# Neighbourhood attention: unscaled weights as the stationary side, sums applied by ScalarE on the way out, and two bias tables that exchange their homes

## The chip, the cores and the metric

The kernel runs on one core of a Trainium2 chip. A core has a matrix engine (TensorE, PE in the rows; its loads of the stationary operand are PEld), VectorE (DVE), ScalarE (ACT), GpSimd (POOL) and a queue that issues transfers (SyncE, SP), with 16 DMA engines behind it. The metric is the time of the program on the device in microseconds (us), the median of several runs. Everything is 32-bit floating point; the trace records each matmul of such operands as two passes.

## The reference

The program is two transformer blocks over 1024 tokens of 1024 features. The part that matters here is half of the second block's mixer:

```python
def neighbourhood_attention(q, k, v, rpb):      # B, T, H, dh = 1, 1024, 8, 64; a grid of 16 rows of 64 tokens
    ...
    scores = jnp.einsum('bhrqd,bhrikd->bhrqik', qg, k_rows) * (dh ** -0.5)   # a row's 64 queries, 8 rows of keys
    scores = jnp.where(in_win[...], scores + bias[None], -jnp.inf)
    p = jax.nn.softmax(scores.reshape(B, H, R, W, KH * W), axis=-1).reshape(B, H, R, W, KH, W)
    return jnp.einsum('bhrqik,bhrikd->bhrqd', p, v_rows)
```

It stands between a gated linear attention in both directions (its other half) and the output projection with the MLP behind it. The softmax divides each query's weights by their sum; that can be done before or after the product with the values.

## The kernel before

The instructions of each engine are written out in a fixed order. The work around the change is written as generators, one per stream of work and engine; `interleave` runs all streams of an engine one step at a time, and `pause(n)` lets a stream skip n steps, so the pauses set the order in which an engine meets the work of different units.

A **unit** is one row of the grid (64 queries) for one pair of heads: 128 partitions (two heads of 64 queries) by 512 keys. There are 16 rows and 4 pairs, 64 units. Eight streams n = 0 to 7 work at once, each with a PSUM bank, a tile of scores `n_sc` and small numbers `n_st`; n below 4 takes the even rows of pair n, the others the odd rows of pair n - 4. Eight units are a **round**, and there are eight rounds. In `near_head` the odd rows have their two heads crossed over, so the four score products of a pair's two units (64 by 64 stationary, 512 columns streamed) lie in the four quarters of the array. Crossed heads need a bias table with its halves exchanged, the turned table.

A unit's chain before: TensorE scores (`near_scores_tensor`, line 3498), VectorE adds the bias, negates and takes the minimum (3462), ScalarE takes the exponential and its sum (3443), VectorE inverts the sum (3465), GpSimd multiplies the weights by it (3480), TensorE turns them in four transposes (line 232, called from `near_values_tensor`), VectorE copies them out (3468), TensorE multiplies them with the values (3519: stationary 128x128 values, 128 turned columns streamed, two heads at once with halves of the result unused), and ScalarE copies the two used quarters of 64x64 over the queries (3449), which is the layout that the output projection reads. A score product of the next round waits for that copy (`mix_out`).

The loads are in `near_loads`, on SyncE's queue: at its end the bias table of the even rows (3136), the values shifted by one row (3138, two halves, for windows that begin at an odd row), and the turned table in two halves of 64 partitions (3142). The even rows' table lies over memory in use until the last projection unit of this attention (`unit_made`), the turned one at U_AT + 96 KB over `la`, the gates of the linear attention, in use until their last prefix sums (`sums_made`, line 3336). VectorE waits for both tables ahead of the attention (top of `neighbourhood`). The weights of the output projection (3740) are issued behind the point where the engines meet (`k.meet()`).

## Time and profile before

| | us |
|---|---|
| median of 3 runs | 3066.36 (3061.49 to 3067.91) |
| the profiled execution | 3066.58 |
| its span, first to last instruction | 3064.4 |
| TensorE busy | 2869.7 (94%) |
| VectorE, ScalarE, GpSimd busy | 1175.4, 596.9, 720.3 |
| mean granted TensorE clock | 0.974 of full speed |
| the neighbourhood attention | 2013.05 to 2171.41 |

Durations come from the one profiled execution. A group's busy time is the union of its instructions, so where they overlap it is below count times mean. "Idle before" names what ended the idle time ahead of an instruction. The clock is a share of 2.4 GHz. In rows of the trace a number behind x counts passes, two for each matmul and one for each transpose; in rows of the program's order it counts instructions.

### The profile page before, as it was taken

To read this page: it belongs to the slowest core of one execution; us is meant where nothing else is said; L and a number is where in the kernel's file an instruction comes from. 1 tells how busy PE (TensorE), PEld (TensorE's weight loads), DVE (VectorE), ACT (ScalarE), POOL (GpSimd) and SP (SyncE) were. 2 spreads that over 40 slices of the span, in tenths; PEclk is the share of its full clock that TensorE was granted. 3 is DMA by queue.
4 is the path that set the end of the run, shared out by engine and by line. 5 is a ranking of instruction groups with operands and counts; after the bars stand their busy time and mean duration, and the time that the engine had idled before them with its cause. 6 is when DMAs were issued, how large, how long until landed. Compare 5 with 4: busy or idle time off the path is not lost.

```text
span 3064.4 us, 30810 instructions
## 1 busy us (share of the span) xinstructions
PE 2869.7 (94%) x12130; PEld 1695.6 (55%) x12130; DVE 1175.4 (38%) x1999; ACT 596.9 (19%) x1223; POOL 720.3 (24%) x544
## 2 busy tenths in 40 slices
PE   7999998988988999999789999969999999999998
PEld 5886544888446666666444455537544444444443
DVE  6715777665132111111143145446633314133142
ACT  4001232322121221121232211125230000000001
POOL 3214565553211000000020000137521122111220
PEclk9999999999998999999899999979999999999999
DMA  8724494000237999999661100040201101111101
GB/s 264 232 45 52 97 249 111 1 28 29 112 137 317 395 426 426 424 426 390 245 221 38 55 1 15 14 132 1 90 28 55 53 30 41 41 55 45 38 28 55
DMA packets 180278, 417.08 MB, mean 136 GB/s; under 512 B 30676, under 2 KB 103828, under 8 KB 170904
## 3 DMA queue, kind: packets, MB, share of 16 engines
q1 hardware_dynamic: 163705, 372.49, 34.3%
q10 hardware_dynamic: 10512, 25.69, 2.6%
q0 software_dynamic: 5904, 16.78, 1.5%
q8 instruction: 101, 1.65, 0.2%
q14 instruction: 56, 0.46, 0.0%
HBM read 374.29 MB, written 59.88 MB: 142 GB/s over the span
## 4 chain that ended last, share of the span: by engine, by line
PE 86%; DVE 6%; DMA 2%; issue 2%; ACT 1%; POOL 1%; SPq 1%; POOLq 0%; ACTq 0%; DVEq 0%
PE bank L3809 27%; PE bank L2554 9%; PE bank L2557 8%; PE bank L748 6%; PE bank L2984 5%; PE bank L1946 4%; PE bank L3161 3%; PE bank L232 3%; PE bank L1266 3%; PE bank L3159 2%; PE bank L883 2%; PE bank L3519 1%; PE bank L1844 1%; PE bank L1841 1%; PE bank L1834 1%
## 5 line engine op out<-in xcount | busy, mean ns | idle before, releaser
L3809 PE MATMUL bank<-w_ff,uT 128*128 128x512 f32 x640 | 276.0, 592 | 0.0
L3809 PE MATMUL bank<-hT,w_ff 128*128 128x512 f32 x512 | 224.3, 596 | 4.3 <-DVE hT L3612 4.3
L3932 DVE TENSOR_TENSOR x_out<-x_out,bank 128x512 f32<-128x512 f32 x140 | 94.7, 687 | 291.5 <-PE bank L3809 291.3
L3809 PEld LDWEIGHTS bank<-w_ff,uT 128*128 128x128 f32 x640 | 121.6, 190 | 153.1 <-issue 153.1
L2554 PE MATMUL bank<-e_w,e_xsT 128*128 128x256 f32 x832 | 184.3, 382 | 1.6 <-DVE e_xsT L2640 1.6
L2557 PE MATMUL bank<-e_w,e_xsT 128*64 128x256 f32 x1408 | 160.8, 388 | 18.5 <-issue 18.5
L2554 PEld LDWEIGHTS bank<-e_w,e_xsT 128*128 128x128 f32 x832 | 158.1, 191 | 32.5 <-issue 11.3
L2984 PE MATMUL bank<-w_gla,nT 128*128 128x512 f32 x384 | 167.1, 595 | 2.4 <-ACT nT L2946 1.3
L3809 PEld LDWEIGHTS bank<-hT,w_ff 128*128 128x128 f32 x512 | 97.5, 191 | 126.3 <-issue 126.0
L3809 PE MATMUL bank<-h_sum,w_ff 128*128 128x512 f32 x384 | 166.1, 592 | 0.0
L2557 PEld LDWEIGHTS bank<-e_w,e_xsT 128*64 128x64 f32 x1408 | 113.2, 140 | 69.8 <-issue 31.2
L2711 DVE TENSOR_TENSOR e_hid<-e_act,bank 128x256 f32<-128x256 f32 x48 | 20.2, 421 | 337.7 <-PE bank L2554 170.4
L3873 POOL TENSOR_TENSOR w_ff<-w_ff,w_ff 128x2048 f32<-128x2048 f32 x9 | 42.7, 4746 | 355.7 <-PE bank L3809 352.5
L3809 PEld LDWEIGHTS bank<-h_sum,w_ff 128*128 128x128 f32 x384 | 73.0, 190 | 91.8 <-issue 91.8
L2984 PEld LDWEIGHTS bank<-w_gla,nT 128*128 128x128 f32 x384 | 72.7, 191 | 92.0 <-issue 88.3
L3161 PE MATMUL bank<-nT,w_nqk 128*128 128x512 f32 x256 | 121.8, 606 | 0.0
L3919 DVE TENSOR_TENSOR uT<-uT,bank 128x512 f32<-128x512 f32 x48 | 33.1, 689 | 229.1 <-PE bank L3809 229.0
L2493 POOL DMA_INDIRECT e_rows<-xn_rows,e_idx x25 | 25.0, 1001 | 405.9 <-PE bank L2523 380.1
L3846 ACT ACTIVATE uT<-bank 128x512 f32<-128x512 f32 x48 | 28.3, 600 | 468.9 <-PE bank L3809 468.9
L748 PE MATMUL bank<-w_in,hT 128*128 128x256 f32 x512 | 115.1, 383 | 0.0
L3480 POOL TENSOR_SCALAR n_sc<-n_sc,n_st 128x512 f32<-128x512 f32 x64 | 99.7, 1564 | 58.3 <-DVE n_st L3465 58.1
L3809 PE MATMUL bank<-w_ff,u_sum 128*128 128x512 f32 x256 | 110.5, 592 | 0.0
(530 smaller groups left out, 4805.1 us busy)
## 6 DMA issues: line engine op xcount, KB each, us to landing
e_w<-in_w SPq DMA_DIRECT2D x108, 2048.0 KB, 22.1
w_ff<-in_w_ff SPq DMA_DIRECT2D x32, 1024.0 KB, 5.2
y_rows<-zero SPq DMA_DIRECT2D x8, 3008.0 KB, 19.0
wa_rest<-in_w_ada SPq DMA_DIRECT2D x32, 512.0 KB, 5.3
y_rows<-e_y ACTq DMA_DIRECT2D x24, 512.0 KB, 9.3
wa<-in_w_ada SPq DMA_DIRECT2D x16, 512.0 KB, 10.8
w_qkv<-in_w_in SPq DMA_DIRECT2D x24, 256.0 KB
w_gla<-in_w_in SPq DMA_DIRECT2D x3, 2048.0 KB, 20.8
```

The source lines that it names most:

```text
L232: t = k.nc.tensor.transpose(bank[:, h * P:(h + 1) * P], src[:, h * P:(h + 1) * P], k.c("ident"))
L748: t = pe.matmul(out, still[:, f, g * P:(g + 1) * P], moving[:, f, :], start=step in (0, 1, 3) and g % 2 == f == 0, stop=f == 3, skip_group ...
L883: t = pe.matmul(k.bank[6 + m % 2][:, :], hT[:, f, m * P:(m + 1) * P], wz[:, f, :], start=f == 0, stop=f == NK - 1)
L1266: t = pe.matmul(conv_bank(k, p, step)[:, :], weights[step][:, f, :], tokens[step](f), start=step in (0, 1, 3) and f == 0, stop=f == 3, ski ...
L1946: t = pe.matmul(k.bank[2 * (m % 2) + h][:, :], mixed, b.w[h][:, f, :], start=f == 0, stop=f == NK - 1)
L2554: return pe.matmul(out, xT, weights[0], start=start, stop=stop)
L2557: t = pe.matmul(out[tokens, :], xT[:, tokens], w, start=start, stop=stop)
L2984: t = pe.matmul(k.bank[3 * (i % 2) + j][:, :], b.nT[:, f, i * P:(i + 1) * P], b.w[at][:, f, :], start=f == 0, stop=f == NK - 1)
L3161: t = pe.matmul(bank[:, :], wqk[c // 2 % 2][:, f, c % 2 * P:(c % 2 + 1) * P], nT[:, f, h * BANK:(h + 1) * BANK], start=f == 0, stop=f == N ...
L3480: g.tensor_scalar(b.sc[n][:, :], b.sc[n][:, :], b.st[n][:, 2:3], None, ALU.mult).then_inc(*s.weights_ready.up().inc)
L3809: t = pe.matmul(bank[:, :], still, moving, start=step in (0, 1, 3) and f == 0, stop=f == 3, skip_group_check=True)
L3932: v.tensor_tensor(dst, dst, k.bank[4 * ((ph + step) % 2) + g][:, :], ALU.add).then_inc(*s.added.up().inc)
```

## The change

1. The weights are turned unscaled, right behind the exponential. GpSimd's part goes.
2. The values product changes sides: the turned weights are the stationary operand (64 queries of one head at a time), the values are streamed (64 features), and the result has queries on its partitions: 8 matmuls a unit in the two column halves of the array, instead of 4 over all of it.
3. ScalarE copies this 128x64 result to a new tile `n_out` and scales it by the inverse sums; TensorE turns it back by two products of 64x64 with the identity; ScalarE copies that, 128x64 in one instruction, over the queries.
4. The bias tables exchange homes: the even rows' table goes to U_AT + 96 KB and is loaded once the last prefix sums of both directions are made; the turned one goes to the other place and is loaded ahead of the shifted values. VectorE waits for each table only at the first unit that reads it.
5. The pauses are new: a round has 12 steps (`NEAR_ROUND`) where it had 8.

```diff
@@ near_areas
-    ... for j, at in enumerate((N_AT + 16 * KB, U_AT + 96 * KB))],
+    ... for j, at in enumerate((U_AT + 96 * KB, N_AT + 16 * KB))],
@@ near_loads
+    for way in gla_s:
+        sy.wait_ge(*way.sums_made(NT))
+    sy.dma_start(near.bias[0][:, :, :], bias_rows).then_inc(*d.bias_got.up().inc)
     sy.wait_ge(*d.unit_made(NT + 4 * PAIRS))
     sy.wait_ge(*d.unit_out(NT))
-    sy.dma_start(near.bias[0][:, :, :], bias_rows).then_inc(*d.bias_got.up().inc)
+    for lo in (0, W):
+        sy.dma_start(near.bias[1][W - lo:P - lo, :, :], bias_rows[lo:lo + W, :, :]).then_inc(*d.bias_turned_got.up().inc)
     ... (the two loads of val_odd, as before)
-    for way in gla_s:
-        sy.wait_ge(*way.sums_made(NT))
-    for lo in (0, W):
-        sy.dma_start(near.bias[1][W - lo:P - lo, :, :], bias_rows[lo:lo + W, :, :]).then_inc(*d.bias_turned_got.up().inc)
@@ neighbourhood
-    k.nc.vector.wait_ge(*d.bias_got(1))
-    k.nc.vector.wait_ge(*d.bias_turned_got(2))
@@ near_start
-    return pause(2 * (n % PAIRS) + n // PAIRS)
+    return pause(NEAR_ROUND // PAIRS * (n % PAIRS) + n // PAIRS)
@@ near_scalar
-        yield from pause(4)
+        yield from pause(2)
         a.wait_ge(*s.neg_max(u + 1))
         a.activation(sc[:, :], sc[:, :], ACT.Exp, scale=-1.0, bias=st[:, 0:1], accum_out=st[:, 1:2]).then_inc(*s.exp_ready.up().inc)
-        yield from pause(4)
+        yield from pause(6)
+        a.wait_ge(*s.sum_inverse(u + 1))
         a.wait_ge(*s.av_made(u + 1))
-        for h in range(2):
-            values, queries = near_head(n, h)
-            m = s.mix_out.up() if h else k.A.up()
-            a.activation(b.qkT[values, p, i * W:(i + 1) * W], k.bank[n][values, queries], ACT.Copy).then_inc(*m.inc)
+        a.activation(b.out[n][:, :], k.bank[n][:, 0:W], ACT.Copy, scale=st[:, 2:3]).then_inc(*s.o_ready.up().inc)
+        yield from pause(2)
+        a.wait_ge(*s.o_turned(u + 1))
+        a.activation(b.qkT[:, p, i * W:(i + 1) * W], k.bank[n][:, W:2 * W], ACT.Copy).then_inc(*s.mix_out.up().inc)
+        yield from pause(2)
@@ near_vector
+        elif u < 2:
+            v.wait_ge(*(d.bias_turned_got(2) if u else d.bias_got(1)))
@@ near_gpsimd: gone
@@ near_values_tensor
-        yield from pause(6)
-        pe.wait_ge(*s.weights_ready(u + 1))
+        yield from pause(4)
         pe.wait_ge(*s.neg_max(u + 1))
+        pe.wait_ge(*s.exp_ready(u + 1))
         transposes(k, bank, b.sc[n]).then_inc(*s.rows_turned.up().inc)
-        yield from pause(2)
+        yield from pause(3)
...
         for q in range(4):
-            t = pe.matmul(bank[:, 0:P], val[:, lo // 2 + q, p * P:(p + 1) * P], b.sc[n][:, q * P:(q + 1) * P], start=q == 0, stop=q == 3)
+            for h in range(2):
+                features, queries = near_head(n, h)
+                t = pe.matmul(bank[queries, 0:W], b.sc[n][:, q * P + queries.start:q * P + queries.stop], val[:, lo // 2 + q, p * P + features.start:p * P + features.stop],
+                              start=q == 0, stop=q == 3)
         t.then_inc(*s.av_made.up().inc)
+        yield from pause(2)
+        pe.wait_ge(*s.o_ready(u + 1))
+        for h in range(2):
+            features, queries = near_head(n, h)
+            t = pe.matmul(bank[features, W:2 * W], b.out[n][queries, :], k.c("ident")[queries, queries], start=True, stop=True)
+        t.then_inc(*s.o_turned.up().inc)
+        yield from pause(3)
```

**TensorE in the middle of the attention, before.** Rows are instructions in the program's order; `n_sc_1_18324` to `18327` are the weights of streams 0 to 3 and `18328` to `18331` those of streams 4 to 7, line 3498 is a pair's scores, line 232 the transposes, line 3519 the values product:

```order
L232 MATMUL bank<-consts_49,n_sc_1_18328 128x128 x4
L3519 MATMUL bank<-n_sc_1_18331,n_val_even_18320 128x128 x4
L3519 MATMUL bank<-n_sc_1_18324,n_val_even_18320 128x128 x4
L232 MATMUL bank<-consts_49,n_sc_1_18325 128x128 x4
L3498 MATMUL bank<-n_qkT_18319 64x512 x4
L3519 MATMUL bank<-n_sc_1_18328,n_val_odd_18321 128x128 x4
L232 MATMUL bank<-consts_49,n_sc_1_18329 128x128 x4
L3519 MATMUL bank<-n_sc_1_18325,n_val_even_18320 128x128 x4
L232 MATMUL bank<-consts_49,n_sc_1_18326 128x128 x4
L3498 MATMUL bank<-n_qkT_18319 64x512 x4
L3519 MATMUL bank<-n_sc_1_18329,n_val_odd_18321 128x128 x4
```

**The same place after the change.** Line 3487 is the scores, 3510 the values product, 3517 the turn back; `n_out_1_18332` to `18335` are the results of streams 0 to 3, `18336` to `18339` those of streams 4 to 7:

```order
L3510 MATMUL bank<-n_val_even_18320,n_sc_1_18324 64x64 x8
L232 MATMUL bank<-consts_49,n_sc_1_18325 128x128 x4
L3517 MATMUL bank<-consts_49,n_out_1_18339 64x64 x2
L3510 MATMUL bank<-n_val_odd_18321,n_sc_1_18328 64x64 x8
L232 MATMUL bank<-consts_49,n_sc_1_18329 128x128 x4
L3517 MATMUL bank<-consts_49,n_out_1_18332 64x64 x2
L3487 MATMUL bank<-n_qkT_18319 64x512 x4
L3517 MATMUL bank<-consts_49,n_out_1_18336 64x64 x2
L3510 MATMUL bank<-n_val_even_18320,n_sc_1_18325 64x64 x8
L232 MATMUL bank<-consts_49,n_sc_1_18326 128x128 x4
L3510 MATMUL bank<-n_val_odd_18321,n_sc_1_18329 64x64 x8
L232 MATMUL bank<-consts_49,n_sc_1_18330 128x128 x4
```

Before, transposes and values products, both over the whole array, stand next to each other between the scores. Now the values products have another shape, and a turn back of two small products stands two or three rows behind each of them, around the scores.

**SyncE's queue at the end of the linear attention, before.** `w_nqk` is the last projection weight of this attention, `n_bias_1_18322` the even rows' table, `n_bias_1_18323` the turned one:

```order
L3133 DMA w_nqk_1_19204<-in_w_in 128x8x256
L3136 DMA n_bias_1_18322<-bias_rows 128x3840
L3138 DMA n_val_odd_18321<-n_val_even_18320 64x4096
L3138 DMA n_val_odd_18321<-n_val_even_18320 64x3584
L3142 DMA n_bias_1_18323<-bias_rows 64x3840 x2
```

**And after the change**, with the waits of the diff ahead of the first and the second table:

```order
L3133 DMA w_nqk_1_19212<-in_w_in 128x8x256
L3136 DMA n_bias_1_18322<-bias_rows 128x3840
L3140 DMA n_bias_1_18323<-bias_rows 64x3840 x2
L3142 DMA n_val_odd_18321<-n_val_even_18320 64x4096
L3142 DMA n_val_odd_18321<-n_val_even_18320 64x3584
```

The turned table has moved ahead of the shifted values; the even rows' table stands where it stood, but waits for something earlier.

## Rows read from the trace of the kernel before

**Rows 1.** stretches: busy us of PE, PEld, DVE, ACT, POOL; PEclk, DMA share, GB/s
```profile
2013.05:2037.72 24.67, 3.69 (x17) 0.80 (x17) 2.78 (x10) 2.73 (x7) 1.64 (x2) 0.50 1.01 247
2037.72:2042.50 4.78, 4.78 (x21) 2.84 (x22) 2.13 (x6) 0.31 (x2) 3.06 (x2) 0.50 1.05 409
2042.50:2171.41 128.91, 123.03 (x990) 91.00 (x989) 84.07 (x243) 75.98 (x248) 95.01 (x61) 1.00 0.01 2
2171.41:3064.40 892.99, 874.71 (x2080) 390.01 (x2080) 306.74 (x328) 73.12 (x136) 184.24 (x68) 0.99 0.14 48
```

**Rows 2.** chain of waits, 1990 to 2200 us: start, us, what
```profile
2008.51 25.32 DMA n_bias<-bias_rows
```

**Rows 3.** timeline, start of the stage: start, us, engine, line, what, idle before
```profile
2034.08 0.69 DVE L3462 CUSTOM_DVE_ANT_0 n_sc<-bank,n_bias 128x512 f32<-128x512 f32 x1 [22.70 <-DMA n_bias<-bias_rows]
2037.72 1.11 PE L232 MATMUL bank<-consts,n_sc 128*128 128x128 f32 x4 [20.98 <-POOL n_sc L3480]
```

**Rows 4.** timeline of TensorE, one round
```profile
2051.64 0.65 PE L232 MATMUL bank<-consts,n_sc 128*128 128x128 f32 x4 [0.64 <-POOL n_sc L3480]
...
2062.05 0.60 PE L232 MATMUL bank<-consts,n_sc 128*128 128x128 f32 x4
2062.48 1.06 PE L3519 MATMUL bank<-n_sc,n_val_even 128*128 128x128 f32 x8
2063.38 0.60 PE L232 MATMUL bank<-consts,n_sc 128*128 128x128 f32 x4
2063.91 1.09 PE L3498 MATMUL bank<-n_qkT 64*64 64x512 f32 x8
2064.93 1.16 PE L3519 MATMUL bank<-n_sc,n_val_even 128*128 128x128 f32 x8
2065.92 0.60 PE L232 MATMUL bank<-consts,n_sc 128*128 128x128 f32 x4
2066.42 1.16 PE L3519 MATMUL bank<-n_sc,n_val_even 128*128 128x128 f32 x8
2068.22 0.66 PE L232 MATMUL bank<-consts,n_sc 128*128 128x128 f32 x4 [0.64 <-POOL n_sc L3480]
```

**Rows 5.** groups by line, 2013 to 2172 us: busy us, mean ns, idle before
```profile
L3480 POOL TENSOR_SCALAR n_sc<-n_sc,n_st 128x512 f32<-128x512 f32 x64 | 99.7, 1564 | 58.3 <-DVE n_st L3465 58.1
L3443 ACT ACTIVATE n_sc<-n_sc,n_st 128x512 f32<-128x512 f32 x64 | 46.0, 720 | 23.4 <-DVE n_st L3462 21.9
L3462 DVE CUSTOM_DVE_ANT_0 n_sc<-bank,n_bias 128x512 f32<-128x512 f32 x64 | 43.7, 684 | 45.2 <-DMA n_bias<-bias_rows 22.7 <-PE bank L3498 22.2 <-issue 0.3
L3468 DVE COPY n_sc<-bank 128x512 f32<-128x512 f32 x64 | 43.4, 687 | 17.4 <-PE bank L232 17.4
L3449 ACT ACTIVATE n_qkT<-bank 64x64 f32<-64x64 f32 x128 | 27.9, 218 | 56.0 <-PE bank L3519 54.0
```

**Rows 6.** short and half-width passes elsewhere: page, timelines, one line's instructions
```profile
L3809 PE MATMUL bank<-w_ff,uT 128*128 128x512 f32 x640 | 276.0, 592 | 0.0
...
1101.21 7.09 PE L2557 MATMUL bank<-e_w,e_hidT 128*64 128x512 f32 x32
1108.23 0.48 PE L2554 MATMUL bank<-e_w,e_xsT 128*128 128x256 f32 x1
...
1130.43 0.20 PEld L2557 LDWEIGHTS bank<-e_w,e_xsT 128*64 128x64 f32 x4 [0.76 <-issue]
...
L1292 PE MATMUL bank<-consts,abT x8: 201/202/223, 358.5 to 358.7; 8*128 8x8 f32 x8
```

**Rows 7.** instructions of the prefix sums: duration ns min/median/max, first and last start
```profile
L3336 PE MATMUL bank<-consts,la x64: 167/251/251, 1764.5 to 1982.4; 128*128 128x2 f32 x64
```

**Rows 8.** landing of line 3136; stretches: us, PEclk, DMA share, GB/s
```profile
DMA to landing us min/median/max: 8.7/8.7/8.7
...
2009.00:2012.00 3.00, 0.97 1.11 415
2024.00:2027.00 3.00, 0.50 1.02 215
```

More of the change, by code:

```diff
@@ L3069 @@
 NEAR_RATE = 1.8
-Near = namedtuple("Near", "qkT val_even val_odd bias sc st")
+Near = namedtuple("Near", "qkT val_even val_odd bias sc out st")
 def gla_tile(k, n):
@@ L3113, in near_areas @@
     return Near(k.at("n_qkT", U_AT + 48 * KB, P, 2 * PAIRS, T), k.at("n_val_even", U_AT + 80 * KB, P, NT, BANK), k.at("n_val_odd", N_AT, P, NT, BANK),
-                [k.at(f"n_bias{j}", at, P, PAIRS, (2 * KH - 1) * W) for j, at in enumerate((N_AT + 16 * KB, U_AT + 96 * KB))],
-                n_sets("sc", U_AT + 112 * KB, NSETS, KH * W), n_sets("st", EARLY_AT + 4 * KB, NSETS, 8))
+                [k.at(f"n_bias{j}", at, P, PAIRS, (2 * KH - 1) * W) for j, at in enumerate((U_AT + 96 * KB, N_AT + 16 * KB))],
+                n_sets("sc", U_AT + 112 * KB, NSETS, KH * W), n_sets("out", EARLY_AT, NSETS, W), n_sets("st", EARLY_AT + 4 * KB, NSETS, 8))
 def near_unit_of(u):
@@ L3395, in neighbourhood @@
 def neighbourhood(k, d, b):
[L3397 to L3399 removed]
+    s = k.on("scored neg_max exp_ready sum_inverse rows_turned pT_out av_made o_ready o_turned mix_out")
     interleave(*(near_scalar(k, s, b, n) for n in NEAR_ORDER))
[L3401 to L3402 removed]
+    interleave(*(near_vector(k, s, d, b, n) for n in NEAR_ORDER))
     interleave(*(near_values_tensor(k, s, d, b, n) for n in NEAR_ORDER), *(near_scores_tensor(k, s, b, p) for p in range(PAIRS)))
@@ L3457, in near_vector @@
         _, dr = near_window(i)
-        yield from pause(3)
+        yield
         v.wait_ge(*s.scored(u // 2 + 1))
@@ L3461, in near_vector @@
             v.wait_ge(*s.av_made(u - NSETS + 1))
+        elif u < 2:
+            v.wait_ge(*(d.bias_turned_got(2) if u else d.bias_got(1)))
         v.tensor_tensor_reduce(sc[:, :], k.bank[n][:, :], b.bias[n // PAIRS][:, p, dr * W:(dr + KH) * W], -1.0, -NEG, ALU.add, ALU.min, st[:, 0:1]).then_inc(*s.neg_max.up().inc)
-        yield from pause(2)
+        yield from pause(3)
         v.wait_ge(*s.exp_ready(u + 1))
         v.reciprocal(st[:, 2:3], st[:, 1:2]).then_inc(*s.sum_inverse.up().inc)
-        yield from pause(2)
+        yield
         v.wait_ge(*s.rows_turned(u + 1))
         v.tensor_copy(sc[:, :], k.bank[n][:, :]).then_inc(*s.pT_out.up().inc)
-        yield
-def near_gpsimd(k, s, b, n):
-    g = k.nc.gpsimd
-    yield from near_start(n)
-    for u, _, _ in near_rows(n):
-        yield from pause(5)
-        g.wait_ge(*s.exp_ready(u + 1))
-        g.wait_ge(*s.sum_inverse(u + 1))
-        g.tensor_scalar(b.sc[n][:, :], b.sc[n][:, :], b.st[n][:, 2:3], None, ALU.mult).then_inc(*s.weights_ready.up().inc)
-        yield from pause(3)
+        yield from pause(7)
 def near_scores_tensor(k, s, b, p):
     pe = k.nc.tensor
-    yield from pause(2 * p)
+    yield from pause(NEAR_ROUND // PAIRS * p)
     for r in range(ROWS // 2):
-        yield from pause(2)
         if r:
@@ L3499, in near_scores_tensor @@
         t.then_inc(*s.scored.up().inc)
-        yield from pause(6)
+        yield from pause(NEAR_ROUND)
 def near_values_tensor(k, s, d, b, n):
@@ L3509, in near_values_tensor @@
         val = b.val_odd if lo % 2 else b.val_even
-        yield from pause(6)
-        pe.wait_ge(*s.weights_ready(u + 1))
+        yield from pause(4)
         pe.wait_ge(*s.neg_max(u + 1))
+        pe.wait_ge(*s.exp_ready(u + 1))
         transposes(k, bank, b.sc[n]).then_inc(*s.rows_turned.up().inc)
-        yield from pause(2)
+        yield from pause(3)
         pe.wait_ge(*s.pT_out(u + 1))
```

7 lines of the change are left out of this document (3 added, 4 removed).

## The prediction

> **What bounds the kernel now.** I read the stretches of the stage by window first, then the chain of waits through it, then TensorE's timeline of one round, then the groups by line. The whole change lies in the neighbourhood attention, from 2013.05 us (the engines meet behind the gated linear attention) to 2171.41 us (first product of the output projection). What follows, 892.99 us with TensorE busy 874.71 of them, starts when the attention ends and only shifts with it [rows 1].
>
> The attention has two parts with different limits. From 2013.05 to 2037.72 us TensorE is busy 3.69 of 24.67 us: it makes the scores of two pairs and then stands [rows 1]. The chain says why: 25.32 us of a transfer of the bias table [rows 2]. VectorE's first instruction on scores starts at 2034.08, after a wait of 22.70 us for it, and TensorE's first turn of weights at 2037.72 [rows 3]. From there on TensorE is the bound: 123.03 of 128.91 us busy at full clock [rows 1]. Its timeline repeats in rounds of 16.58 us (2051.64 to 2068.22), with one gap in each: the transposes at 2068.22 waited 0.64 us for GpSimd [rows 4], which scales the weights, 1.56 us a unit [rows 5]. From 2066.42 to 2068.22 TensorE does 0.90 us of products, so a round loses 0.90 us and holds 15.68 us of work.
>
> **What that work is made of.** Steps between starts in [rows 4]: four transposes between work of the same shape 0.43 us (2062.05 to 2062.48), the values product of a unit 0.90 us (2062.48 to 2063.38; 8 passes, 0.111 each), a pair's scores 1.02 us (2063.91 to 2064.93). The scores are two waves of a 512-column pass, and such a pass is 0.431 us (276.0 over 640 [rows 6]), so 0.86. The rest is the price of using the array in another shape: transposes ahead of scores take 0.53 instead of 0.43, scores 1.02 instead of 0.86, products behind scores 0.99 instead of 0.90 (2064.93 to 2065.92). That is 0.35 us for two changes, 0.175 each. The experts' half-width work shows 7.02 us for 32 passes in two column halves (1101.21 to 1108.23), 16 x 0.431 = 6.90 for the streaming, so 0.12 for a way out [rows 6]. I take 0.16 per change, bounds 0.10 and 0.175. The same 32 passes show that two column halves do run side by side.
>
> **The change, part by part.**
> *The start.* The table of the even rows waits now only for the last prefix sums of both directions, 1982.4 us [rows 7], instead of 2006.3; it took 8.7 us to land [rows 8], so it is there by 1992, under the linear attention. The turned table is issued at 2006.3 with nothing ahead of it. It moves at half the speed of the full one: 415 GB/s while the full table runs, 215 while a turned half runs [rows 8]. Its 1.97 MB take 9.2 us; with 1 us before the first packet and 1.5 us behind the last it lands at about 2018.0. Bounds: 2015.0, if it moved like the full one, and 2025, if the odd values, issued right behind, took half of the engines. Odd values and projection weights come behind it; the first odd row is two rounds away, so they are hidden. The first unit needs the early table alone: its transposes can start at about 2016.9 (scores 1.9 at the slow clock, reduction 0.7, exponential 0.9, signals). The second needs the turned one: reduction 2018.1 to 2018.8, exponential to 2019.6 [rows 5], transposes at 2019.7. Dense work thus starts at 2019.7 instead of 2037.72: 18.0 us won.
> *The clock* is at 0.50 when the stage opens and rose 4.8 us after the work had become dense (2037.72 to 2042.50) [rows 1]. The same 4.8 us, a loss of 2.4, come again: no gain, no loss.
> *GpSimd's 64 multiplications go.* They were on the path once a round: 0.90 us back, against new small waits for which I allow 0.2. VectorE inverts the sums as before.
> *The values product* becomes 8 instructions a unit, 16 passes in 8 pairs, the two of a pair in the two column halves, with 64 stationary and 64 streamed columns each. No such pass is in the trace. From below: half of a 128-column pass, 0.055 us a pair. From above: 0.111 a pair, as a pass of today, if the halves don't overlap. Near: eight passes of 8 streamed columns, alternating between two row groups, start within 0.2 us (358.5 to 358.7), 0.07 a pair at most, and four loads of 64 columns, two per half, are over in 0.20 us, the length of one included [rows 6]. I take 0.06: 0.48 us a unit, 3.84 a round, where there were 8 x 0.89 = 7.1.
> *The turn back* is added: 2 instructions, two pairs of small passes, 0.12 us a unit, 0.96 a round.
> *Changes of shape.* The new order [the order rows in the section on the change] alternates full width (transposes), half width (values) and quarters (scores, turn back). Over a full round of it I count 22 changes, before 8: 22 x 0.16 = 3.52 us.
> A round: scores 4 x 0.86 = 3.44, transposes 8 x 0.43 = 3.44, values 3.84, turn back 0.96, changes 3.52: 15.2 us of work, 15.4 with the new waits. (Before: 3.44 + 3.44 + 7.1 + 8 x 0.175 = 15.4, measured 15.68.) The cheaper products pay for the changes of shape and for little more.
> *ScalarE* had an exponential and two 64x64 copies a unit (0.72 and 2 x 0.218 [rows 5]); now the copies are 128x64, which I price 0.23 (bounds 0.218 and 0.30). Some 1.2 us a unit, 9.4 a round, lie under TensorE's 15.4; VectorE's reduction and copy, 0.684 each, stay. The chain of a unit (scores 1.1, reduction 0.7, exponential 0.9, transposes 0.6, copy 0.7, values 0.8, scaled copy 0.4, turn 0.4, copy 0.4) is 6 us plus signals, and the order leaves a twelfth of a round, 1.3 us, or more at each hand-over. Uncovered, a late copy costs its 0.23 us at each of 64 turns, 15 us; that is how B below comes about.
>
> **The sum.** 8 rounds x 15.2 = 121.6, less the first transposes and two scores, done by 2019.7 (2.6): 119.0. Plus 2.4 clock, 1.6 new waits, 2.0 for the tail. The end comes at 2019.7 + 125.0 = 2144.7 instead of 2171.4: 26.7 us less. The same count for before, 2037.72 + 8 x 15.68 - 2.6 + 2.4 + 7 x 0.90 = 2169.3, leaves 2.1 for its tail, so the way of counting closes. The profiled execution took 3066.58 us (span 3064.4, 2.2 around it), 0.2 above the median of 3066.36. Forecast: 3066.4 - 26.7 = 3040.
>
> **Rivals.**
> A. *The column halves don't overlap in such short passes.* A pair then costs 0.111, at 80 pairs a round 4.1 us more, 32.6 over 8 rounds: 5.9 us slower than now, 3072. It decides from 0.10 us a pair on, where the 26.7 are used up. For it: four queued instructions in 0.06 us, which no row shows sustained. Against: [rows 6].
> The Trainium skill, "TensorE: Matmul & The Clock Gate", LDWEIGHTS, prices a load by its columns, 53 ns for 64; loads in single file would make 107 ns a pair and this rival. The four loads in 0.20 us speak against single file.
> B. *The longer chain holds the round at its old length.* ScalarE's queue has the scaled copy and the last copy between exponentials, and TensorE waits for both. If that eats all of the round's gain, 8 x (16.58 - 15.4) = 9.4 us come back: 3049.
> C. *The turned table lands at 2025*: 7 us come back: 3047.
> D. *A floor per pass adds up.* 96 more passes a round (160 against 64), at 0.025 us each (eight starts within 0.2 us [rows 6]): 2.4 us a round, 19 in all: 3059. For it: the passes are as short as any in the trace. Against: those eight stream 8 columns each and cost the floor and no more, so it reads as a floor under a pass, not on top of it.
> The skill's "TensorEngine Tiling", Instruction Overhead, is this rival's rule: some 60 cycles for each matmul, and no tiling of a dimension that is small already.
>
> **How the numbers follow.** Forecast 0.58, A 0.11, B 0.16, C 0.08, D 0.07. The lower end: 0.055 a pair and 0.10 a change give a round of 13.5, 14 us less than forecast: 3026. Both upper bounds together give 3077, which is A and more. The range 3026 to 3064 takes in B, C and D and leaves out A and a little. A measurement of this kernel tells 0.2%, 6 us, from no change. Faster by more (below 3060.2): forecast, B, C and part of D, less what I may have missed: 0.85; within 0.05; slower 0.10.
>
> **What would show it.** VectorE's first reduction near 2015 us and the second near 2018, with a DMA wait of 2 to 3 us between; nothing on GpSimd; rounds of about 15.4 us with TensorE busy throughout; values passes in pairs 0.06 us apart; ScalarE's 128x64 copies near 0.23 us. I am wrong if pairs lie 0.11 us apart, if ScalarE is the releaser of TensorE in each round, if the granted clock falls below 1.0 inside the stage, or if dense work starts after 2022.

## The result, and the profile after

The changed kernel takes 3037.39 us (median of 4 runs, 3036.02 to 3037.81) against 3067.14 for the kernel before on the same chip (3061.49 to 3068.89): ratio 0.9905, 95% interval 0.989 to 0.9921, so 29.7 us or 1% less. The forecast was 3040 us.

The first view is the same as in [rows 1], the stage cut at the places that answer to those of before: opening to the first transposes of unit 1, from there to the clock's return, the rest, and what follows. Columns: window, its length, busy time (instructions) of PE, PEld, DVE, ACT, POOL, then PEclk, DMA share, GB/s.

```profile
2018.64:2025.22 6.58, 4.44 (x21) 1.37 (x21) 2.40 (x8) 1.78 (x5) 0.00 (x0) 0.68 1.01 206
2025.22:2029.60 4.38, 4.38 (x36) 2.46 (x38) 2.42 (x9) 2.39 (x7) 0.00 (x0) 0.62 1.03 217
2029.60:2142.38 112.78, 112.21 (x1740) 76.86 (x1738) 83.26 (x242) 70.45 (x245) 0.00 (x0) 1.00 0.12 42
2142.38:3035.30 892.92, 874.53 (x2080) 390.12 (x2080) 306.72 (x328) 73.03 (x136) 184.38 (x68) 0.99 0.14 48
```

The stage takes 123.74 us (2018.64 to 2142.38) instead of 158.36, 34.6 less. What follows is as long as before. The span shrank by only 29.1 us because this execution opened the stage 5.6 us later. 3.7 of these are there long before the changed code: the experts' first products, line 2557, start at 1000.1 us instead of 996.4. In the 14 profiled executions of the two kernels and the experiments they start between 994.6 and 1011.1 us, and the stage opens between 2012.49 and 2029.42 (four of the experiments also move the opening by their own edit, as told there). Whether such a shift belongs to the execution or to the program isn't shown: the four runs of the changed kernel lie within 1.8 us of each other. A median carries some microseconds of this, so below I compare the length of the stage as well. It comes from one profiled execution of each kernel; how well it repeats wasn't measured, but kernels with the same operations in the same order have the same rounds (14.68 us in two of them, 16.57 and 16.58 in two others).

The start, in the timelines of VectorE and TensorE of the changed kernel (start, us, engine, line, what, idle before and its releaser), answers to [rows 3]:

```profile
2020.81 0.69 DVE L3464 CUSTOM_DVE_ANT_0 n_sc<-bank,n_bias 128x512 f32<-128x512 f32 x1 [4.14 <-PE bank L3487]
2023.52 0.69 DVE L3464 CUSTOM_DVE_ANT_0 n_sc<-bank,n_bias 128x512 f32<-128x512 f32 x1 [2.02 <-DMA n_bias<-bias_rows]
```

And TensorE's, over the same microseconds:

```profile
2018.64 3.69 PE L3487 MATMUL bank<-n_qkT 64*64 64x512 f32 x16 [0.81 <-ACTq L164]
2022.56 0.74 PE L232 MATMUL bank<-consts,n_sc 128*128 128x128 f32 x4 [0.23 <-ACT n_sc L3441]
2025.22 0.63 PE L232 MATMUL bank<-consts,n_sc 128*128 128x128 f32 x4 [1.91 <-ACT n_sc L3441]
```

The 22.70 us for the table have become 2.02 for its turned half, and dense work begins 6.58 us after the opening instead of 24.67. A piece of a steady round (14.68 us from 2063.60 to the same place at 2078.28) answers to [rows 4]:

```profile
2063.60 0.28 PE L3517 MATMUL bank<-consts,n_out 64*64 64x64 f32 x2
2063.62 0.65 PE L3487 MATMUL bank<-n_qkT 64*64 64x512 f32 x2
2063.71 0.23 PE L3517 MATMUL bank<-consts,n_out 64*64 64x64 f32 x2
2063.76 1.03 PE L3487 MATMUL bank<-n_qkT 64*64 64x512 f32 x6
2064.53 0.29 PE L3517 MATMUL bank<-consts,n_out 64*64 64x64 f32 x4
2064.75 0.69 PE L3510 MATMUL bank<-n_val_even,n_sc 128*64 128x64 f32 x16
2065.36 0.66 PE L232 MATMUL bank<-consts,n_sc 128*128 128x128 f32 x4
2065.95 0.69 PE L3510 MATMUL bank<-n_val_odd,n_sc 128*64 128x64 f32 x16
...
2068.86 0.33 PE L3517 MATMUL bank<-consts,n_out 64*64 64x64 f32 x4
2069.12 0.69 PE L3510 MATMUL bank<-n_val_even,n_sc 128*64 128x64 f32 x16
```

No row has a gap in brackets. TensorE never waits in a round; the 0.57 us missing from 112.78 in the third row of the first view are two waits at the very end. A values product takes 0.61 us from its start to the next work's (2064.75 to 2065.36) where [rows 4] has 0.90. Pass by pass, its two column halves start within 7 ns of each other, and the pairs follow each other by 58 ns, 107 behind the first. The turn back's first passes start at 2063.60, the scores' at 2063.62 and its next at 2063.71, although they stand ahead of the scores in the queue: the two run among each other. Scores and two turn backs together take 1.15 us (2063.60 to 2064.75) where scores alone take 1.02, and a turn back between other work 0.26 (2068.86 to 2069.12), which has one more change of shape in it.

TensorE's clock, in a finer cut of the first two rows (columns as in the first view):

```profile
2022.50:2025.22 2.72, 0.75 (x5) 0.57 (x5) 1.70 (x6) 0.96 (x3) 0.00 (x0) 0.94 0.95 193
2025.22:2026.20 0.98, 0.98 (x8) 0.59 (x12) 0.98 (x5) 0.56 (x2) 0.00 (x0) 1.00 1.32 267
2026.20:2029.60 3.40, 3.40 (x32) 1.86 (x26) 1.44 (x5) 1.83 (x5) 0.00 (x0) 0.50 0.95 202
```

It rose to 2.4 GHz early in the first of these rows, behind 3.69 us of scores and before the work was dense. It fell back to 1.2 GHz 1 us after the dense work had begun, behind TensorE's wait of 1.91 us, stayed there for 3.4 us, and was up from then on.

The groups of the stage, answering to [rows 5] (busy us, mean ns, idle before):

```profile
L3441 ACT ACTIVATE n_sc<-n_sc,n_st 128x512 f32<-128x512 f32 x64 | 46.0, 719 | 26.0 <-DVE n_st L3464 24.1
L3445 ACT ACTIVATE n_out<-bank,n_st 128x64 f32<-128x64 f32 x64 | 19.8, 309 | 19.5 <-PE bank L3510 18.8 <-DVE n_st L3467 0.8
L3448 ACT ACTIVATE n_qkT<-bank 128x64 f32<-128x64 f32 x64 | 13.3, 211 | 3.6 <-PE bank L3517 3.6
L3517 PE MATMUL bank<-consts,n_out 64*64 64x64 f32 x256 | 19.9, 237 | 0.2 <-ACT n_out L3445 0.2
```

The scaled copy takes 309 ns, more than either copy of before; the idle time beside it is ScalarE waiting for TensorE, so it hides.

### The profile page after: what moved, and what is told of

The parts are those of the page before. It is cut to its first block, busy times and chain, and to the rows that moved or that the text cites. A ratio compares the mean times of both kernels' runs of the same rounds, so it can differ in the third digit from the quotient of the medians.

```text
span 3035.3 us, 32282 instructions
## 1 busy us (share of the span) xinstructions
PE 2865.1 (94%) x12898; PEld 1687.8 (56%) x12898; DVE 1179.5 (39%) x1999; ACT 592.7 (20%) x1223; POOL 618.4 (20%) x480
## 4 chain that ended last, share of the span: by engine, by line
PE 88%; DVE 6%; issue 2%; DMA 2%; ACT 1%; POOL 1%; SPq 0%; ACTq 0%; DVEq 0%; POOLq 0%
PE bank L3808 28%; PE bank L2554 9%; PE bank L2557 8%; PE bank L748 6%; PE bank L2984 5%; PE bank L1946 4%; PE bank L3161 3%; PE bank L232 3%; PE bank L1266 3%; PE bank L3159 2%; PE bank L883 2%; PE bank L1844 1%; PE bank L3510 1%; PE bank L1841 1%; PE bank L1834 1%
## 5 line engine op out<-in xcount | busy, mean ns | idle before, releaser
L2554 PEld LDWEIGHTS bank<-e_w,e_xsT 128*128 128x128 f32 x832 | 158.5, 192 | 32.7 <-issue 11.3
L748 PEld LDWEIGHTS bank<-w_in,hT 128*128 128x128 f32 x512 | 97.8, 192 | 14.9 <-issue 1.7
## 6 DMA issues: line engine op xcount, KB each, us to landing
y_rows<-zero SPq DMA_DIRECT2D x8, 3008.0 KB, 18.8
```

The source lines that it names most:

```text
L748: t = pe.matmul(out, still[:, f, g * P:(g + 1) * P], moving[:, f, :], start=step in (0, 1, 3) and g % 2 == f == 0, stop=f == 3, skip_group ...
L2554: return pe.matmul(out, xT, weights[0], start=start, stop=stop)
```

## The experiments

For each I give the median and, from its profiled run, the length of the stage (first scores to the output projection's first product).

**One half of the change each.** The bias tables alone, put on the kernel before:

```diff
+    for way in gla_s:
+        sy.wait_ge(*way.sums_made(NT))
+    sy.dma_start(near.bias[0][:, :, :], bias_rows).then_inc(*d.bias_got.up().inc)
     sy.wait_ge(*d.unit_made(NT + 4 * PAIRS))
...
+        elif u < 2:
+            v.wait_ge(*(d.bias_turned_got(2) if u else d.bias_got(1)))
```

> The kernel before with the bias tables' part of the change alone: homes exchanged, the even table loaded early, the turned one ahead of the odd values, VectorE's waits moved to units 0 and 1. Theory: the two parts add up, and this one is worth what the first transposes come earlier. They start 24.67 us after the stage opens before and 6.58 us after it in the changed kernel, so the stage (158.36 us before) becomes about 140.3, and the time 3067.1 - 18 = 3049 us (3046 to 3052). The rounds stay at 16.58 us with GpSimd's waits in them. Rival: the long start lets later units catch up (all scores are there when the tables land), so an early table only spreads the first round's work and wins at most what TensorE stood idle; the stage then becomes 148 or more and the time 3055 or more.

Measured: 3051.82 us (3049.17 to 3053.59), ratio 0.9939 (0.9923 to 0.9956). Its timeline:

```profile
2014.34 3.69 PE L3498 MATMUL bank<-n_qkT 64*64 64x512 f32 x16 [0.81 <-ACTq L164]
2021.98 1.12 PE L232 MATMUL bank<-consts,n_sc 128*128 128x128 f32 x4 [3.95 <-POOL n_sc L3480]
...
2155.22 14.00 PE L3809 MATMUL bank<-w_ff,n_qkT 128*128 128x512 f32 x32 [0.58 <-ACTq L164]
```

The stage is 140.88 us, 17.5 less than before, and the steady rounds are the old 16.57. Theory right by the stage and the rounds. The other half, the changed kernel with homes, loads and waits as before:

```diff
-    for way in gla_s:
-        sy.wait_ge(*way.sums_made(NT))
-    sy.dma_start(near.bias[0][:, :, :], bias_rows).then_inc(*d.bias_got.up().inc)
     sy.wait_ge(*d.unit_made(NT + 4 * PAIRS))
     sy.wait_ge(*d.unit_out(NT))
+    sy.dma_start(near.bias[0][:, :, :], bias_rows).then_inc(*d.bias_got.up().inc)
...
+    k.nc.vector.wait_ge(*d.bias_got(1))
+    k.nc.vector.wait_ge(*d.bias_turned_got(2))
```

> The changed kernel with the bias tables' homes, loads and waits as they were before: the unscaled weights, the product with column halves, the scaling copy and the turn back alone. Theory: the start stays as before (first transposes 24 to 25 us after the opening), the rounds are 14.68 us long instead of 16.58 and the tail 7.8 instead of 11.9, so the stage is 158.4 - 7 x 1.9 - 4.1 = 141 us and the time about 3050 us (3046 to 3054). Rival: the prediction's forecast of 15.4 us a round was right and the shorter round of the changed kernel comes from the staggered start that the two tables give (scores and turn backs beside each other because the units are apart in time); with all units starting together rounds are 15.4 or longer, and the time is 3056 or more.

Measured: 3056.13 us (3054.84 to 3060.13), ratio 0.9955 (0.9938 to 0.9971). The stage is 141.43 us (2019.27 to 2160.70), 16.9 less than before, with rounds of 14.68: as expected, while the median is 2 us over the range. The stage doesn't explain that; this execution opened it at 2019.27, 6.2 us later than the kernel before. The two halves add up: 17.5 + 16.9 = 34.4 of the 34.6.

**Do the two column halves run side by side?** The loops exchanged, so that neighbours in the queue share a half:

```diff
-        for q in range(4):
-            for h in range(2):
-                features, queries = near_head(n, h)
+        for h in range(2):
+            features, queries = near_head(n, h)
+            for q in range(4):
```

> The changed kernel with the loops of the values product exchanged: first the four passes of one head, then the four of the other, so that passes next to each other lie in the same half of the columns. The output is unchanged. Theory: the two halves of a pair run side by side (a pair takes 0.058 us, a pass alone 0.055 or more), and one after the other they cost 8 x 0.055 instead of 4 x 0.058 in a unit: 0.21 us more, 1.7 in a round, 13 in the stage: 3050 us (3045 to 3055). If a pass in one half costs 0.111, 0.65 a unit and 3079 us. Rival (cost goes by the columns alone, nothing runs side by side: a pass costs 0.029 wherever it lies): 3037 us, no change.

Measured: 3056.6 us (3056.12 to 3062.02), ratio 0.9959 (0.9945 to 0.9973); stage 143.17 us, 19.4 more than the changed kernel's, rounds 16.92. From its timeline:

```profile
2079.87 0.97 PE L3510 MATMUL bank<-n_val_even,n_sc 128*64 128x64 f32 x16
2080.76 0.66 PE L232 MATMUL bank<-consts,n_sc 128*128 128x128 f32 x4
```

The same 16 passes take 0.89 us instead of 0.61: 0.28 a unit. The rival (cost by columns alone) is out. The passes of one half start 0.058 us apart, which is what a pair takes in two halves. I had counted 8 passes where there are 16: with 16, full single file would have been 0.46 a unit more. It came out at 0.28 because this order isn't full single file either: the second head's passes begin 0.29 us behind the first head's (2079.87 and 2080.16), with three of the first's still to start. Even so the narrow product now costs what the wide one did before (0.90, [rows 4]; 0.15 of the 0.89 is the change of shape behind it): all the product wins is the company of the other half.

**Is it the turned side, or the width?** The kernel before with the product in halves and nothing else:

```diff
-            t = pe.matmul(bank[:, 0:P], val[:, lo // 2 + q, p * P:(p + 1) * P], b.sc[n][:, q * P:(q + 1) * P], start=q == 0, stop=q == 3)
+            for h in range(2):
+                features, queries = near_head(n, h)
+                t = pe.matmul(bank[features, queries], val[:, lo // 2 + q, p * P + features.start:p * P + features.stop],
+                              b.sc[n][:, q * P + queries.start:q * P + queries.stop], start=q == 0, stop=q == 3)
```

> The kernel before with nothing but its values product cut in column halves: values stay the stationary side, now 64 features of one head at a time, against 64 columns of that head's weights; GpSimd's multiplication, ScalarE's two copies and the tables' start stay. The product of a unit goes from 4 passes of 128x128 (0.222 us each) to 8 of 128x64 (0.058 a pair). Theory: what the change saves in the product is the width, not the turned side; TensorE's own work in a round falls from 15.68 to about 13.5 us. GpSimd's multiplications take 8 x 1.56 = 12.5 us of it and stand in each unit's chain, so some of the gain turns into waits: a round of 14 to 15.2 us, 7 x 2 = 14 us less in the stage: 3053 us (3046 to 3058). Rival: the units' chains through GpSimd set the round already (its waits are 0.9 us a round before), and the freed time becomes waiting: 16.4 us a round and 3065 us or more.

Measured: 3064.07 us (10 runs, 3059.5 to 3069.72), ratio 0.9981 (0.9968 to 0.9993); stage 148.41, 10.0 less than before, rounds 15.30. Between theory and rival, and the median above the theory's range: of the stage's 10.0 us only some 5 arrived in it, and this execution opened the stage at 2026.43. Its timeline says why:

```profile
2077.97 0.69 PE L3521 MATMUL bank<-n_sc,n_val_even 128*64 128x64 f32 x16 [0.22 <-DVE n_sc L3468]
2079.77 0.66 PE L232 MATMUL bank<-consts,n_sc 128*128 128x128 f32 x4 [1.12 <-POOL n_sc L3480]
```

TensorE's product is as short as in the changed kernel (0.69 for x16), so the width makes it short and not the turned side. But the waits for GpSimd grew from 0.90 to some 1.6 us a round (here 1.19 between 2078.58 and 2079.77, and 0.43 at another unit), and VectorE's copy adds 0.3. They eat part of what the width frees.

**GpSimd's place by itself.** In the kernel before the multiplication is cut to 8 columns; the weights are therefore not scaled:

```diff
-        g.tensor_scalar(b.sc[n][:, :], b.sc[n][:, :], b.st[n][:, 2:3], None, ALU.mult)
+        g.tensor_scalar(b.sc[n][:, 0:8], b.sc[n][:, 0:8], b.st[n][:, 2:3], None, ALU.mult)
```

> The kernel before with GpSimd's multiplication cut from 512 columns to 8 (all else, waits too, stays; the output isn't scaled). It prices GpSimd's place in the chain alone. Theory: TensorE's waits for GpSimd go (0.90 us in each of 7 steady rounds, 3 to 4 us in the tail, 1.5 at the start), TensorE's own 15.68 us a round stay: the stage is 10 to 12 us shorter, 3058 us. Rival (the unit's chain through VectorE and ScalarE takes GpSimd's place, as the wait's last entry): rounds stay above 16.2 us and the time above 3064.

Measured: 3058.31 us (6 runs, 3056.2 to 3061.04), ratio 0.9968 (0.9956 to 0.998); stage 148.94, 9.4 less; rounds 15.62, and no wait for GpSimd after the first. The 0.90 us a round were real (16.57 to 15.62 is 0.95), and nothing took its place; the stage won a little less than the 10 to 12 us of the theory.

**The turn back's price.** In the changed kernel each is done twice:

```diff
-        for h in range(2):
+        for h in (0, 1, 0, 1):
```

> The changed kernel with each turn back done twice in a row (the second writes the same numbers). It prices the turn back's passes without its changes of shape. Theory: half of the turn backs start beside the scores and the pairs follow each other every 0.055 to 0.1 us; two more pairs are 0.11 to 0.2 us a unit, less where they lie beside the scores: 0.8 to 1.2 us a round, 6 to 9 us: 3045 us. Rival A: they vanish beside the scores, under 2 us in all: 3037 to 3039. Rival B: the turn back is as dear as its isolated 0.26 us shows: 2.1 a round, 16 us: 3053.

Measured: 3051.95 us (3048.67 to 3057.03), ratio 0.9941 (0.9924 to 0.9958); stage 131.43, 7.7 more than the changed kernel's; rounds 15.68, 1.00 more, so 0.125 us for the second turn back of a unit. Theory right by the stage and the round. The second turn back costs about the same everywhere: 0.11 to 0.14 us beside the scores (a visit with one unit's turn back is 1.24 us for 1.13, with two units' 1.42 for 1.15), 0.12 between other work (0.38 for 0.26). So the scores hide part of a first turn back, and next to nothing of a second. The median is 7 us higher than the stage explains; the profiled run, the slowest of the four at 3057.03, opened at 2029.42, the latest of all, and the other three are 3 to 8 us faster.

**Changes of shape, and a better order.** The changed kernel's operations in another order (a table of slots in place of the pauses), two products, two transposes, two turn backs and the scores for each pair:

```diff
+NEAR_ROUND = 24
+NEAR_SLOTS = {"bias": (2, 3), "exp": (4, 6), "inverse": (5, 7), "turn": (10, 11), "turned": (10, 12), "values": (14, 15), "scale": (15, 17), "back": (18, 18), "out": (20, 21)}
```

> The changed kernel with all its operations, in another order: the two units of a pair side by side, so that TensorE runs scores, two values products, two transposes, two turn backs for each pair, in place of alternating. Theory (a change of shape costs 0.10 to 0.16 us on TensorE): four changes fewer from product to transposes and four fewer from transposes to product in a round, 8 x 0.14 = 1.1 us less: 13.6 us a round, stage 8 us shorter, 3029 us (3026 to 3033). Rival: TensorE runs into VectorE and ScalarE, whose work now comes in pairs (8 x 1.61 = 12.9 and 8 x 1.43 = 11.4 us a round), and stands idle for what it saves: 3037 or more.

Measured: 3029.01 us (3026.91 to 3031.43), ratio 0.9869 (0.9853 to 0.9886); stage 112.25, rounds 13.02. One pair:

```profile
2073.82 0.69 PE L3521 MATMUL bank<-n_val_even,n_sc 128*64 128x64 f32 x16
2074.34 0.64 PE L3521 MATMUL bank<-n_val_odd,n_sc 128*64 128x64 f32 x16
2074.90 1.09 PE L232 MATMUL bank<-consts,n_sc 128*128 128x128 f32 x8
2075.93 0.34 PE L3528 MATMUL bank<-consts,n_out 64*64 64x64 f32 x8
2076.09 1.04 PE L3497 MATMUL bank<-n_qkT 64*64 64x512 f32 x8
2077.06 0.69 PE L3521 MATMUL bank<-n_val_even,n_sc 128*64 128x64 f32 x16
```

The theory's mechanism is right and its size was too small: the round is 1.66 us shorter and the stage 11.5, where it had 1.1 and 8. It counted eight changes fewer; the rows show ten, since the turn backs lie beside the scores in every pair: 22 become 12, and 10 x 0.16 is 1.6. That the median is the forecast 3029 is luck: this execution opened the stage at 2021.59, 2.9 us later than the changed kernel's. And the same order with the values stationary in halves, scaling by GpSimd and no turn back:

```diff
+                t = pe.matmul(bank[features, 0:W], val[:, lo // 2 + q, p * P + features.start:p * P + features.stop],
+                              b.sc[n][:, q * P + queries.start:q * P + queries.stop], start=q == 0, stop=q == 3)
...
+        a.activation(b.qkT[:, p, i * W:(i + 1) * W], k.bank[n][:, 0:W], ACT.Copy).then_inc(*s.mix_out.up().inc)
```

> The bias tables as in the changed kernel, but the weights scaled by GpSimd and the values as the stationary side, in column halves, both heads' results in one 64-column stretch (so one copy by ScalarE and no turn back); and TensorE's order in each pair of units is scores, both values products, both transposes, instead of alternating. Theory: TensorE needs 1.09 us for two products in a row (as the halves-only kernel's trace has it), about 1.03 for two units' transposes and 1.0 for the scores, so 3.15 a pair and 12.6 a round; VectorE then has 8 x (0.68 + 0.08 + 0.15 + 0.69) = 12.9 us of work in a round and GpSimd 12.5, so VectorE binds at 12.9 to 13.4 instead of TensorE's 14.68. 7.5 rounds' worth x 1.5 = 11 us: about 3026 us (3022 to 3032). Rival (GpSimd in the chain): three engines within 3% of each other and 1.56 us of GpSimd between exponent and transposes make waits of 1.5 us a round or more, as in the halves-only kernel (1.4), and the time is 3037 or more.

Measured: 3023.65 us (3022.71 to 3025.2), ratio 0.9852 (0.9836 to 0.9869), the fastest of all: 13.7 us under the changed kernel by the medians, 13.5 by the stage (110.21); rounds 12.50. One pair of it on TensorE:

```profile
2072.15 1.09 PE L3507 MATMUL bank<-n_qkT 64*64 64x512 f32 x8
2073.17 0.69 PE L3531 MATMUL bank<-n_sc,n_val_even 128*64 128x64 f32 x16
2073.68 0.64 PE L3531 MATMUL bank<-n_sc,n_val_odd 128*64 128x64 f32 x16
2074.25 1.09 PE L232 MATMUL bank<-consts,n_sc 128*128 128x128 f32 x8
2075.27 1.09 PE L3507 MATMUL bank<-n_qkT 64*64 64x512 f32 x8
```

And 70 us of steady rounds (columns as in the first view):

```profile
2050.00:2120.00 70.00, 70.00 (x1068) 46.03 (x1065) 61.31 (x180) 39.54 (x134) 69.51 (x46) 1.00 0.01 2
```

A period is 3.12 us without a gap. 8 units of 8 pairs at 0.058 (3.71) + 3.44 for scores + 3.44 for transposes are 10.59; the other 1.91 of the round's 12.50 are 12 changes of shape at 0.16. The changed kernel's own steps show the same price: a product takes 0.61 us for 0.46 of passes, four transposes 0.59 for 0.43, scores 1.02 for 0.86. 20 changes between transposes, products and scores make 3.2, and 10.59 + 3.2 leave 0.89 of its 14.68 for 8 turn backs with all their own changes. By the timeline it is 1.00: six beside the scores add 0.47 to four visits of 1.02, two between other work take 0.26 each. In the paired order a round with turn backs is 0.52 longer than one without (13.02 against 12.50): 0.065 a unit, two units' turn backs side by side in four quarters, just ahead of the scores. My expectation named VectorE as the next bound, from a sum of durations; it is busy 61.31 of 70, and GpSimd, at 69.51, is the engine that is nearly full. It holds nobody up: the order leaves a third of a round (8 slots of 24) between its multiplication and the transposes.

**The start: attempts, none of use.** First, the projections that run beside the gated attention handed out faster:

```diff
-NEAR_RATE = 1.8
+NEAR_RATE = 2.0
```

> The changed kernel with one number changed: the projections that fill the gated attention's gaps are handed out 2.0 a step instead of 1.8, so that the last one, on which the turned table's load waits, is done some 8 steps earlier. Theory: the turned table is issued 5 us or more before the 7 us ahead of the opening at which it is now, and lies there when unit 1 asks; the first 6.6 us of the stage lose 2 to 4, and the time is 3034 us (3032 to 3036). Rival: the projections covered the waits of the last gated rounds; without them TensorE stands idle there for as long as the start wins, and the time is 3037 or more.

Measured: 3044.49 us (3042.96 to 3045.41), ratio 0.9921 (0.9905 to 0.9938), 7 us more than the changed kernel. The stage did shrink, to 120.96, but the rival won:

```profile
2021.16 1.11 PE L232 MATMUL bank<-consts,g_o 128*128 128x128 f32 x4 [5.58 <-DVE g_o L3260]
2025.09 1.11 PE L232 MATMUL bank<-consts,g_o 128*128 128x128 f32 x4 [2.81 <-DVE g_o L3260]
```

Without projections to cover them TensorE waits 8.4 us for VectorE before these two transposes, instead of 4.6, and 4.7 more in the rounds before them (at lines 3375, 3353 and 3363), where the changed kernel has none. Second, the copies of the odd values held back until the turned table is there:

```diff
         sy.dma_start(near.bias[1][W - lo:P - lo, :, :], bias_rows[lo:lo + W, :, :]).then_inc(*d.bias_turned_got.up().inc)
+    sy.wait_ge(*d.bias_turned_got(2))
```

> The changed kernel with one wait more in the queue of loads: the odd values are copied only when the turned table has landed. Theory (what ends the start is the table's second half, whose 11.3 us from issue to landing are shared with the copies of the odd values; alone it takes about 7 to 8): VectorE's wait of 2.0 us for it goes, unit 1's transposes start about 4.5 us after the opening instead of 6.58, and the copies still land 15 us or more before round 2 asks for them. 2 us in the stage, 3035 us. Rival A: the halves are slow for their 64 partitions and not for the company, nothing moves: 3037. Rival B: the odd values come too late: round 2 waits, 3040 or more.

Measured: 3041.15 us (3037.75 to 3044.62), ratio 0.9913 (0.9899 to 0.9926), 4 more than the changed kernel. TensorE's timeline at the opening:

```profile
2022.81 3.69 PE L3488 MATMUL bank<-n_qkT 64*64 64x512 f32 x16 [7.47 <-SPq L164]
```

And the landing of the three loads of bias tables, from the view of that tile:

```profile
DMA to landing us min/median/max: 7.2/7.3/11.2
```

Both say that I was wrong. The last half lands 11.2 us after its issue (11.3 in the changed kernel), with or without the odd values beside it: rival A's mechanism. And all engines meet before the stage (line 164), SyncE too: the wait that I put in its queue moved the 7 us ahead of the opening, for everybody. I had not looked at who waits for that queue. The stage itself is 120.94, 2.8 shorter, since the table lies there when it opens. The same wait on the paired kernel:

> The paired-order kernel (scaling by GpSimd, values stationary in halves) with the same wait more. Theory: as with the changed kernel, the first unit that uses the turned table starts 2 us earlier, and GpSimd, busy all the time from its first multiplication on, moves with it: 3021.5 us against 3023.65. Rival: GpSimd's queue takes up the 2 us, 3023 to 3024.

Measured: 3029.3 us (3021.34 to 3031.49), ratio 0.9875 (0.986 to 0.989), against 3023.65 without. The profiled run is the fastest, 3021.34; the other three took 3028.29 or more, and no trace tells why. The stage is 106.08, 4.1 shorter, and TensorE waits 7.04 us for SyncE ahead of it in place of 0.81: neither of the two numbers held. Last, dummy products on top of that kernel:

```diff
+    for n in (2, 2, 1, 3, 4, 3, 4, 0, 0):
+        for _ in range(n):
+            pe.matmul(k.bank[6][:, 0:P], k.c("ident"), k.c("ident"), start=True, stop=True)
+        yield
...
+        for _ in range(11 if u == 0 else 0):
+            pe.matmul(k.bank[PAIRS - 1][:, 0:P], k.c("ident"), k.c("ident"), start=True, stop=True)
```

> The kernel of the run before it, with 30 dummy products (128x128 by 128x128, written to a free bank and read by nobody) where TensorE waits: 5 and 14 of them before the gated attention's last two transposes, 11 before the first transposes of the stage. Theory: TensorE's clock fell to half for 7.6 us after the start's idle time in the paired-order kernel (granted 0.56 from 2027.10 to 2034.66, and 0.72 in the 7.75 us ahead); kept busy, it stays at 1.0, and the 7.1 us of work done there take about 4: 3 us less, 3018.5 us. Rival: the clock isn't what sets the pace of the start (the table, VectorE and GpSimd are), and the dummies only fill: no change, or up to 2 us more where they stand in the way.

Measured: 3026.57 us (3024.48 to 3027.17), ratio 0.9862 (0.9847 to 0.9877). By stretches (columns as above):

```profile
2012.00:2020.00 8.00, 4.61 (x38) 4.01 (x36) 2.70 (x8) 1.37 (x2) 1.25 (x2) 0.98 1.01 217
2020.00:2028.00 8.00, 3.34 (x16) 1.04 (x20) 1.18 (x3) 0.38 (x1) 0.00 (x0) 0.50 0.64 131
2028.00:2034.00 6.00, 6.00 (x49) 3.81 (x42) 4.04 (x17) 4.18 (x12) 5.17 (x4) 0.84 0.95 212
```

The first dummies held the clock at 0.98 until 4.7 us before the opening; without them it is 0.75 over the same stretch, 12.7 to 4.7 us before it. Then, in the 7.75 us at the engines' meeting, it fell to 0.50 anyway. The last dummies put the first transposes at 7.87 us after the opening instead of 5.81, and the stage is 106.87, 0.8 longer. By the stage the rival is right: they stood in the way. The medians can't decide it: 3026.57 is 2.7 below the kernel without dummies, well within that kernel's spread of 10 us. Whether a warm clock helps where no such meeting follows stays open.

## Why the prediction was right, and where its terms were off

**The start** was right in mechanism and size. Dense work starts 6.58 us after the opening; forecast was 2019.7 against an opening at 2013.05, 6.65. The second reduction starts 4.88 us after the opening (forecast 5.0), behind a DMA wait of 2.02 (forecast 2 to 3). 18.09 us are won, 18.0 were forecast, and the bias-only kernel shows 17.5 by itself. Rival C is out: the turned table was there 11.9 us after its first half's issue (2011.5 to 2023.4), for which the step had 11.7, and the odd values behind it took nothing.

**The round** came out at 14.68 us instead of 15.2 of work and 15.4 with waits. From the start of dense work to the end the changed kernel takes 117.16 us (2025.22 to 2142.38); forecast were 125.0. These 7.8 us are, by term:
- Work, 8 x 0.52 = 4.2 us. The values product was 3.84 and is 3.71 (pairs 0.058 apart for the 0.06 that I took). The turn back was 0.96, and two of the 22 changes of shape were counted for it (0.32); with its changes it costs 0.89 by difference, 1.00 by the timeline. This is one step whose mechanism I had missed: its passes run among the scores', so that two turn backs around a pair's scores add 0.13 us and not 0.24. The price of a change, 0.16, and their number, 22, were right.
- New waits, 1.6 us: there are none.
- The clock, 0.7: it was at half for 3.4 us of dense work (0.62 over 4.38 us, in the second row of the first view), not 4.8. The mechanism was another, too: I had it at half from the opening until it rises for good, but it rose before the dense work and fell back 1 us into it. One of my signs of being wrong, a clock below 1.0 inside the stage, so came true, at a cost of 1.7 us where 2.4 were in the sum.
- The tail, 1.4: forecast 2.0, left are 0.6, by difference.

**GpSimd gone.** 0.95 us a round, as the short multiplication shows (16.57 to 15.62), for the 0.90 forecast. **ScalarE's copies** were under-priced: 0.309 for the scaled one, above my upper bound of 0.30, and 0.211 for the last one, 0.52 a unit where I had 0.46. It cost nothing: ScalarE waits 18.8 us for TensorE before the scaled copies. Rival B, the longer chain, is thereby out.

**Rival A** would have needed single file, and there is none in the changed kernel. Its price was right: passes in one half follow each other every 58 ns, so a pair in single file is 0.116 us, for which it had 0.111. The exchanged loops lose 19.4 us of stage and not 32.6 because three passes of eight still overlap there, and because the rival counts the turn backs too. Full single file would be, by estimate, 0.46 us more in each of 64 products, 30 us, and some 7 more for the turn backs: a stage of about 161 us against 158.4 before. "Slower than before" was thus a sound reading of a case that didn't occur; no run has it. The Trainium skill, "TensorE: Matmul & The Clock Gate", LDWEIGHTS, prices a load of 64 columns at 53 ns, which would put 107 ns into a pair in single file. Inside one half the trace comes near that, 58 ns; but the halves don't queue behind each other, since pairs of the changed kernel follow each other every 58 ns, too. **Rival D**, a floor that adds up, is out by the same rows: twice the passes, 0.61 us instead of 0.90.

**The sum.** Forecast −26.7, the stage's measure −34.6, of which 29.7 arrived in the medians. The start gave its 18 us; what follows it was to give 8.7 and gave 16.5, almost twice as much: 4.2 of the difference by the rounds' work, 3.7 by waits, clock and tail. The distance to 3040 is small because some 5 us of the stage's gain were lost ahead of it, for a reason that stays open and that nothing in the prediction had foreseen. So the mechanism was right, and the closeness of the number is luck in part. One slip without effect: both upper bounds together give 3075, not 3077.

## What to carry to other kernels

Narrow passes paid here only where neighbours in the queue lay in different parts of the array: order the loops so that they do. A second operation can hide among quarter-array work in part (two turn backs for 0.13 us instead of 0.24). Each change of shape had a price of about 0.16 us, so grouping equal shapes of two units shortened the stage by 11.5 us, a third of what the whole change brought, and the medians by 8. And before a wait is put into a queue, look who meets that queue further on.

## What the runs showed of the hardware

- Passes of 64x64 in different quarters start among each other: a turn back's passes at 2063.60 and 2063.71 us around the scores' at 2063.62. Around a pair's scores two turn backs add 0.13 us and one adds 0.11 (1.15 and 1.13 against 1.02). Between other work one takes 0.26, of which 0.16 is a further change of shape.
- Passes of 128x64 stationary by 64 streamed columns start every 58 ns in one column half (exchanged loops), and in pairs every 58 ns in two (changed kernel).
- A change between full width, column halves and quarters costs 0.15 to 0.16 us: a product takes 0.61 us for 0.46 of passes, four transposes 0.59 for 0.43.
- A scaled copy of 128x64 from a bank takes 309 ns, an unscaled one 211.
- The even table, one load over 128 partitions, landed 7.2 us after its issue; the turned one, as many bytes in two loads of 64 partitions each, 11.9 us after the first's, and the odd values' copies beside it made no difference (11.3 and 11.2 us for the second load).
